# A two-layer encoder on one core: norm sums as two fp32r passes of a high and a low part, and a first block loaded and multiplied in small pieces

## The reference

```
h   = RMSNorm(x);  z = h @ W_in -> [q_a | kv_a | k_rope | B | C | conv_in]
attention on low-rank q and kv (both normed), conv = B * conv3(C * conv_in)
mix = concat(norm per head(attn), norm per group(conv)) @ W_out
x  += RMSNorm(mix)
x  += RMSNorm(W_down relu(W_up RMSNorm(x))^2)
x  += RMSNorm(sigmoid(RMSNorm(x) @ W_g) * (p[i] @ W_p))
```

## Time and profile before

| | |
|---|---|
| time, median of 3 runs | 2851.69 us (2851.42 to 2854.39) |
| the profiled execution | 2853.73 us, its span 2851.9 us |
| PE busy | 2794.9 us, 98% of the span |
| DVE, ACT busy | 1716.5 us (60%), 1203.5 us (42%) |
| share of PE in the chain that ended last | 93% |
| mean granted clock of PE | 0.995 |

### The profile page before, as it was taken

The page is one execution under the profiler, slowest core; times in us unless marked ns, Lnnn a source line. Parts: engine busy times, 40 slices in busy tenths (PEclk is TensorE's granted clock), DMA queues, the critical chain, the costliest instruction groups (busy, mean ns, idle before and its releaser), DMA issues.

```text
span 2851.9 us, 34891 instructions
## 1 busy us (share of the span) xinstructions
PE 2794.9 (98%) x13184; PEld 2307.4 (81%) x13184; DVE 1716.5 (60%) x2300; ACT 1203.5 (42%) x1917; POOL 114.2 (4%) x105
## 2 busy tenths in 40 slices
PE   6999999999999999999999999999999999999996
PEld 5888888888888888888887888888888888888885
DVE  4367888465444544458765588883844454444776
ACT  4236778553111211226643377774621121121473
POOL 0221000000000000000013200000000000000000
PEclk9999999999999999999999999999999999999998
DMA  4121111521111111112332111133211111111232
GB/s 150 60 74 48 32 31 26 212 79 52 59 44 44 57 39 51 45 66 97 103 109 74 57 39 33 28 137 114 88 52 44 44 56 40 51 44 44 76 102 74
DMA packets 62731, 190.73 MB, mean 67 GB/s; under 512 B 7968, under 2 KB 7968, under 8 KB 62624
## 3 DMA queue, kind: packets, MB, share of 16 engines
q1 hardware_dynamic: 62624, 189.29, 20.0%
HBM read 166.13 MB, written 23.13 MB: 66 GB/s over the span
## 4 chain that ended last, share of the span: by engine, by line
PE 93%; ACT 2%; DMA 2%; DVE 2%; SPq 1%; issue 1%; ACTq 0%; DVEq 0%
PE ps L825 28%; PE ps L827 28%; PE ps L826 28%; PE ps L992 3%; PE ps L1017 2%; PE ps L1016 2%; DMA raw<-w_units 1%; DMA mix_lo<-yl 1%; PE ps L1026 1%; PE ps L871 0%; PE ps L893 0%; PE ps L864 0%; ACT hh L1261 0%; ACT pr L1441 0%; PE ps L957 0%
## 5 line engine op out<-in xcount | busy, mean ns | idle before, releaser
L825 PE MATMUL ps<-hh,wh 128*128 128x512 f32 x2192 | 871.6, 398 | 28.1 <-DVE wl L1649 24.2
L827 PE MATMUL ps<-hh,wl 128*128 128x512 f32 x2192 | 855.5, 390 | 0.0
L826 PE MATMUL ps<-hl,wh 128*128 128x512 f32 x2192 | 855.4, 390 | 0.0
L825 PEld LDWEIGHTS ps<-hh,wh 128*128 128x128 f32 x2192 | 412.9, 188 | 122.7 <-issue 31.4
L826 PEld LDWEIGHTS ps<-hl,wh 128*128 128x128 f32 x2192 | 413.0, 188 | 93.1 <-issue 8.6
L827 PEld LDWEIGHTS ps<-hh,wl 128*128 128x128 f32 x2192 | 412.7, 188 | 86.6
L1261 ACT ACTIVATE wh<-raw 128x1024 fp32r<-128x1024 f32 x244 | 254.8, 1055 | 382.7 <-PE ps L827 369.9
L1992 DVE TENSOR_TENSOR xf<-xf,ps 128x512 f32<-128x512 f32 x464 | 310.7, 684 | 146.1 <-PE ps L827 145.5
L825 PE MATMUL ps<-gh,wh 128*128 128x512 f32 x1024 | 398.6, 389 | 0.0
L827 PE MATMUL ps<-gh,wl 128*128 128x512 f32 x1024 | 398.4, 389 | 0.0
L826 PE MATMUL ps<-gl,wh 128*128 128x512 f32 x1024 | 398.3, 389 | 0.0
(11 more groups left out here) (139 smaller groups left out, 3021.6 us busy)
## 6 DMA issues: line engine op xcount, KB each, us to landing
raw<-w_units SPq DMA_DIRECT2D x240, 512.0 KB, 3.3
hh<-mix_hi SPq DMA_DIRECT2D x14, 512.0 KB, 6.2
hl<-mix_lo SPq DMA_DIRECT2D x14, 512.0 KB, 7.0
stage<-w_head SPq DMA_DIRECT2D x16, 320.0 KB, 3.0
xf<-x_in SPq DMA_DIRECT2D x4, 1024.0 KB, 9.0
mix_hi<-cyh SPq DMA_DIRECT2D x8, 512.0 KB, 2.6
mix_lo<-cyl SPq DMA_DIRECT2D x8, 512.0 KB, 3.8
sq<-sums SPq DMA_DIRECT2D x32, 128.0 KB, 2.8
```

The lines of the kernel that those rows point to most:

```text
L825: nc.tensor.matmul(dst, ah, bh, start=start, stop=False)
L826: nc.tensor.matmul(dst, ah, bl, start=False, stop=False)
L827: return nc.tensor.matmul(dst, al, bh, start=False, stop=stop)
```

## The change

Three things are done.

First, 28 norm sums are no longer one float32 matmul but two fp32r matmuls, of the total's high part and its low part (`two_passes`). For each one ACT gets a copy of the total (`post_high`, `pre_high`, or a copy in the input stage), and behind it DVE a subtraction (`post_low`, `pre_low`). They are seven border norms in layer 0 (the table `TWO_PASSES`), five in layer 1 (the two that only serve a next layer or its own end stay as they were), and in each layer four latent sums and four of the convolution. `STATS_AT` is the same as before; only latent sum 1 moves one output later (`LSTAT_AT` 17 to 18, with its neighbours).

Second, the first block is done in pieces. SP loads units 2 and 3 into the idle buffer `bb` beside units 0 and 1, x comes in quarters of a half between them, and the constants come behind. PE works through units and chunks in eight pieces by `first_part`, with the norm sum ahead of the last 36 matmuls. The squares of x (t = 0) are taken after all chunks.

Third, the ones come through a small copy on DVE (`ones_r`), and waits on `w_in` count one load less, since two loads go past `raw`.

```
+TWO_PASSES = [("post", 0, 0), ("pre", 0, 0), ("post", 0, 1), ("pre", 0, 1), ("pre", 1, 1), ("pre", 2, 0), ("post", 2, 1)]
-LSTAT_AT = [15, 17, 21, 23]
+LSTAT_AT = [15, 18, 21, 23]
@@ MIX_ACT
-copy_out.7 square_out.7 copy_out.8 square_out.8 copy_out.9 square_out.9 high.30 post.0.0 copy_out.10
+copy_out.7 square_out.7 copy_out.8 square_out.8 copy_out.9 square_out.9 high.30 post_high.0.0 post.0.0 copy_out.10
...
@@ sync
-            load(0, 0)
-            load(0, 1)
-            sp.dma_start(cst[:, :, :], consts).then_inc(const_in, 16)
-            load_x(0)
-            load(0, 2)
-            load(0, 3)
-            for i in range(1, 4):
-                load_x(i)
+            load(0, 0)
+            load_x(0)
+            load(0, 1)
+            load_x(1)
+            load_beside(0)
+            load_x(2)
+            load_beside(1)
+            load_x(3)
...
@@ tensor
+            def two_passes(dst, ones, hi, lo):
+
+                nc.tensor.matmul(dst, ones.bitcast(f32r), hi, start=True, stop=False)
+                return nc.tensor.matmul(dst, ones.bitcast(f32r), lo, start=False, stop=True)
...
             def post_stats(L, k, t):
...
-                nc.tensor.matmul(ps[:, 6, :], ones, accy[:, t, :], start=True, stop=True).then_inc(post_stat, 1)
+                total = total_at(L, "post", k, t)
+                if total:
+                    pe.wait_ge(total_lo, total)
+                    two_passes(ps[:, 6, :], ones_r[:, 0, :], rpre_r[:, 1, :], accy_r[:, t, :]).then_inc(post_stat, 1)
...
-                    side_by_side([(n, n) for n in range(SLOTS)], 0, pre_ready(R, 0), in_out)
+                    first_part(0, range(2))
+                    first_part(1, range(2))
+                    first_part(0, range(2, 4))
+                    first_part(1, range(2, 4))
+                    first_part(2, range(4))
+                    first_part(0, range(4, DC)).then_inc(in_out, 1)
+                    first_part(1, range(4, DC)).then_inc(in_out, 1)
+                    pe.wait_ge(const_in, 48)
+                    pe.wait_ge(stage_lo, 1)
                     pre_stats(L, -1, 0)
+                    first_part(2, range(4, DC)).then_inc(in_out, 1)
+                    first_part(3, range(DC)).then_inc(in_out, 1)
@@ scalar
+            def high_of_total(L, kind, k, t):
+
+                group = (L + 1, "pre", -1, t) if (kind, k) == ("pre", 2) else (L, kind, k, t)
+                act.wait_ge(*sum_at(last_of(*group)))
+                copy(rpre_r[:, t if kind == "pre" else 1, :], sum_of(group + (0,))).then_inc(total_hi, 1)
@@ vector
+            def low_of_total(L, kind, k, t):
+
+                dve.wait_ge(total_hi, total_at(L, kind, k, t))
+                part = (sum_r if kind == "pre" else accy_r)[:, t, :]
+                whole = (xacc, tmp)[t][:, :] if kind == "pre" else accy[:, t, :]
+                low(part, whole, rpre_r[:, t if kind == "pre" else 1, :]).then_inc(total_lo, 1)
```

More of the change, by code:

```diff
@@ L118 @@
 CHUNKS = CONV // P
+FIRST_AT = [0, 2, 4, 6]
+TWO_PASS = 2
 def taker_of(w):
@@ L836, in unit_output, with first_part @@
                 return last
[L838 to L846, removed]
+            def first_part(n, part):
+                unit_ready(0, n)
+                for k in part:
+                    pe.wait_ge(pre_lo, pre_at(0, -1) * 16 + k + 1)
+                    last = split_product(ps[:, n, :], wh[:, n, k, :], wl[:, n, k, :],
+                                         hh[:, k, hs(0)], hl[:, k, hs(0)], k == 0, k == DC - 1)
+                return last
             def two_tiles(bank, slot, m, moving_hi, moving_lo, start=True, stop=True):
@@ L863, in pre_stats @@
                     pe.wait_ge(pre_ln, pre_at(L, k) * 2 + 1)
-                nc.tensor.matmul(ps[:, 7, :], ones, (xacc, tmp)[t][:, :], start=True, stop=True).then_inc(pre_stat, 1)
+                total = total_at(L - 1, "pre", 2, t) if k < 0 else total_at(L, "pre", k, t)
+                if total:
+                    pe.wait_ge(total_lo, total)
+                    two_passes(ps[:, 7, :], ones_r[:, 0, :], rpre_r[:, t, :], sum_r[:, t, :]).then_inc(pre_stat, 1)
+                else:
+                    nc.tensor.matmul(ps[:, 7, :], ones, (xacc, tmp)[t][:, :], start=True, stop=True).then_inc(pre_stat, 1)
             def post_stats(L, k, t):
@@ L870, in post_stats @@
                     pe.wait_ge(post_ln, post_at(L, k) * 2 + 1)
-                nc.tensor.matmul(ps[:, 6, :], ones, accy[:, t, :], start=True, stop=True).then_inc(post_stat, 1)
+                total = total_at(L, "post", k, t)
+                if total:
+                    pe.wait_ge(total_lo, total)
+                    two_passes(ps[:, 6, :], ones_r[:, 0, :], rpre_r[:, 1, :], accy_r[:, t, :]).then_inc(post_stat, 1)
+                else:
+                    nc.tensor.matmul(ps[:, 6, :], ones, accy[:, t, :], start=True, stop=True).then_inc(post_stat, 1)
             def stats_at(L, *where):
@@ L1344, in _ @@
             for c in range(DC):
-                if c % 4 == 0:
-                    split_unit(0, c // 2)
-                    split_unit(0, c // 2 + 1)
+                if c in FIRST_AT:
+                    split_unit(0, FIRST_AT.index(c))
                 if c == 0:
-                    act.wait_ge(const_in, 32)
+                    act.wait_ge(gains_first, 16)
                 pre_chunk(None, -1, 0, c)
+            for c in range(DC):
+                square((0, "pre", -1, 0, c), x[:, 0, c, :])
             for L in range(DEPTH):
@@ L1383, in _ @@
                                 square((L, "lora", i, i // 2, c), zr[:, c, hs(i // 2)])
+                    for i in range(4):
+                        if LSTAT_AT[i] - 1 == n:
+                            act.wait_ge(*sum_at(last_of(L, "lora", i, i // 2)))
+                            if i == 0:
+                                act.wait_ge(pre_stat, pre_at(L, -1) * 2 + 2)
+                            copy(sum_r[:, i % 2, :], accy[:, i % 2, :]).then_inc(lr_sum_hi, 1)
                     for j in range(CHUNKS - 1):
@@ L1388, in _ @@
                                 nc.scalar.activation(cvs[:, t2, :], cv[:, hs(t2)], ACT.Square).then_inc(cv_sq, 1)
+                            for t2 in range(2 if j < TWO_PASS else 0):
+                                act.wait_ge(cv_sq, L * 8 + 2 * j + t2 + 1)
+                                copy(cvr_r[:, t2, :], cvs[:, t2, :]).then_inc(cv_sq_hi, 1)
                         if CSTAT_AT[j] + 1 == n:
@@ L1830, in _ @@
                             conv_gate(j)
+                        if MULT_AT[j] + 1 == n and j < TWO_PASS:
+                            for t2 in range(2):
+                                dve.wait_ge(cv_sq_hi, L * 2 * TWO_PASS + 2 * j + t2 + 1)
+                                low(cvs_r[:, t2, :], cvs[:, t2, :], cvr_r[:, t2, :]).then_inc(cv_sq_lo, 1)
+                    for i in range(4):
+                        if LSTAT_AT[i] - 1 == n:
+                            dve.wait_ge(lr_sum_hi, L * 4 + i + 1)
+                            low(accy_r[:, i % 2, :], accy[:, i % 2, :], sum_r[:, i % 2, :]).then_inc(lr_sum_lo, 1)
                     if n == 33:
```

147 lines of the change are left out of this document (98 added, 49 removed).

## The result

The changed kernel takes 2830.06 us (median of 4 runs, 2828.62 to 2831.45), the kernel before in the same comparison 2852.56 (4 runs, 2851.42 to 2854.39). The ratio is 0.9920, interval 0.9903 to 0.9938. The forecast was 2830.7.

What follows compares the result with a forecast made beforehand. PE was taken to bound the kernel. Span 2851.9 - 19.1 (first block) - 11.7 (sums) + 9.5 (stalls) + 0.3 = 2830.9, 21.0 less; on the median, 2830.7 us. Own range 2827 to 2835, over the cases 2824 to 2841.

Steps and rivals of the forecast that it cites:

- four stalls: First post norm (t = 0) 3.2 us and MLP pre norm (t = 1) 1.55 us, in both layers: 9.5 us lost.
- unit 4's first matmul earlier: End of the first block: unit 4 starts at 33.5 instead of 49.68, 16.2 us gained.
- clock behind the first block: Behind the first block PE no longer idles, so the clock should not fall: 2.9 us more gained.
- 28 two-pass sums: Border norms, latent and convolution sums: 0.45 us instead of 0.87, gain 0.42 each, 11.7 us in all.
- small rest: First convolution sums: PE may wait for their parts, no more than 0.3 us per layer; 0.3 added in the sum.
- What bounds the kernel: Whole kernel: PE busy 2794.9 of 2851.9 us; its listed waits were two for a low weight part, 24.2 us.
- The rival by which the pairs save nothing: All 28 sums: two passes as dear as one float32 matmul, 2842.4 us; chance 0.03.
- the one by which each pair is waited for: All 28 sums: each waits 1.55 us, 43.4 lost against 30.8 gained, 2864 us; chance 0.03.
- The clock behind a stall: First post norm, both layers: rival that the clock falls in the new stall, 2.9 us each, 2836.5 us; chance 0.09.
- The first block: Kernel start: PE starts at about 8.2, has data throughout and no idle before unit 4; 19.1 us gained with the clock.
- the margin of the ones: First norm sum: its wait for ones_r and the constants has the smallest margin of the start, 1.9 us.
- The rule of the Trainium skill that was set against this part: First block: a stream stopping for a transfer at every tile falls to the lower clock, so pieces would not reach 2.4 GHz.

Runs made afterwards that it cites:

- both parts ahead: Changed kernel with post_high.0.0, post_low.0.0 and pre_low.0.1 moved ahead of high.30, low.30 and value.2.0 in both layers; 2816.62 us, ratio 0.9872.
- the norm sum last: Changed kernel with the input's first norm sum behind the first block's last piece, not ahead of its last 36 matmuls; 2836.50 us, ratio 0.9942.

## Why the prediction was right, and where two errors cancelled

The differences below are from the trace of the changed kernel against that of before, at the same product matmul. Only at the four stalls, where two or three effects fall together, are they taken apart by the experiments: the price of the sums is from the kernels with all sums plain and with both parts ahead, the clock's from the two waits behind which it stayed up.

| term | forecast | measured |
|---|---|---|
| unit 4's first matmul earlier | -16.2 | -17.2 |
| clock behind the first block | -2.9 | -2.9 |
| 28 two-pass sums | -11.7 | -12.4 |
| four stalls | +9.5 | +10.4 |
| clock behind two of the stalls | 0 | +3.2 |
| unit 25's split | not seen | -4.4 |
| small rest: convolution in the forecast, attention in the trace | +0.3 | -0.8 |
| sum | -21.0 | -24.1 (the span: -24.0) |

**What bounds the kernel** held. Each jump in the difference of the traces is one in PE's waits, in the price of a sum, or in its clock. But the list of PE's waits was not as short as the prediction has it. The kernel before had these too:

```profile
PE ps L871 <- DVE accy L1679: 7.5, 1, 7.5
PE ps L825 <- ACT pr L1441: 5.8, 6, 2.1
```

The first is at the kernel's end and did not change; the second is where unit 25's split counts. The last row but one of the table lies in waits for `kl` in the attention, which move by 0.3 us each even between two executions of the changed kernel; it is not explained further.

**Two-pass sums.** Right in kind and a little too small. A pair takes two ordinary steps, 0.45 us, at 24 places of the changed kernel and at all 28 with both parts ahead. The plain sum costs 0.91, not the 0.87 that was read from the earlier trace rows: the reading ended at 120.10, and the next eight matmuls still stand slightly wider apart than 0.227. In the kernel before:

```profile
122.17 0.39 PE L827 MATMUL ps<-hh,wl 128*128 128x512 f32 x1
```

From 118.09 to here are 14 ordinary distances and the sum: 4.08 - 14 x 0.2267 = 0.91 (0.2267 is the 0.68 / 3 of the earlier trace rows unrounded), and the traces with and without two passes come to rest 0.45 apart. In the convolution, where plain sums stand in pairs, the gain is 0.42 to 0.43 each. The rival by which the pairs save nothing is out, and so is the one by which each pair is waited for.

**The stalls.** The step was right in place and cause, and nearly in size. PE's starts stand 3.55 and 1.86 us apart (560.68 to 564.22, 643.22 to 645.08), so 3.32 and 1.63 are lost at once where 3.2 and 1.55 were forecast. The first matmuls behind a wait also stand slightly wider apart, so that by the traces the places cost 3.4 and 1.8 in the end. Here is the first, in the changed kernel:

```profile
560.68 0.39 PE L871 MATMUL ps<-hh,wl 128*128 128x512 f32 x1
561.16 1.06 ACT L1332 ACTIVATE wh<-raw 128x1024 fp32r<-128x1024 f32 x1 [4.24 <-PE ps L871]
562.12 0.61 ACT L1332 ACTIVATE rpre_r<-accy 128x512 fp32r<-128x512 f32 x1
562.25 1.22 DVE L1743 TENSOR_TENSOR wl<-raw,wh 128x1024 fp32r<-128x1024 f32 x1 [4.60 <-ACT wh L1332]
563.39 0.68 DVE L1743 TENSOR_TENSOR accy_r<-accy,rpre_r 128x512 fp32r<-128x512 f32 x1
...
564.22 0.60 PE L901 MATMUL ps<-rpre_r,ones_r 128*128 128x512 f32 x1 [3.16 <-DVE accy_r L1743]
...
564.62 0.63 PE L902 MATMUL ps<-accy_r,ones_r 128*128 128x512 f32 x1
```

The rows show the whole chain: ACT stands idle for 4.24 us before the unit's copy, which waits for an output of PE, the high part stands behind it, DVE does the unit's low part first, and PE waits for the last of them. And the second:

```profile
643.22 0.39 PE L871 MATMUL ps<-hh,wl 128*128 128x512 f32 x1
643.64 0.69 DVE L2088 SCALAR_TENSOR_TENSOR stage<-ps,rpre 128x512 f32<-128x512 f32 x1 [3.09 <-PE ps L871]
644.25 0.68 DVE L1743 TENSOR_TENSOR sum_r<-tmp,rpre_r 128x512 fp32r<-128x512 f32 x1
...
645.08 0.47 PE L901 MATMUL ps<-rpre_r,ones_r 128*128 128x512 f32 x1 [1.47 <-DVE sum_r L1743]
```

**The clock behind a stall** is the step that failed in kind. The forecast took 0 and gave the mechanism a chance of 0.09 as a rival, since no row told of a shorter idle stretch than 4.78 us. It came true in both layers; the pair behind the first stall is shown with 0.60 and 0.63 us a matmul, where an ordinary one has 0.39. Its price was too high, though: 3.68 - 9 x 0.227 = 1.6 us in the stretch, and 1.6 against each of the two waits behind which the clock stayed, not 2.9, because the lower clock lasted 3.4 us here and 6.8 at the earlier trace rows. Over all traces with the wait of 3.16 us (the changed kernel twice, and three experiments) the clock fell behind 9 of 10 such waits. Behind the waits of 1.5 us it did not fall in the changed kernel. The trace of before could have told that much, though no more: it has a wait of 2.07 us, in the row for `pr` that the prediction left out, and behind it the clock stayed at 1.00:

```profile
1917.74 0.47 PE L825 MATMUL ps<-hh,wh 128*128 128x512 f32 x1 [2.07 <-ACT pr L1441]
```

**The moved split of unit 25** is the step that was left out. It was in the diff of the lists, and the wait was in the trace of before (PE waited 5.8 us for `pr` in six places), but I had gone through the lists only for the 28 sums. It gains 4.4 us; together with the clock's 3.2 lost it leaves the total near the forecast by accident. The smaller misses, 1.0 us too little for the first block, 0.7 for the sums and 0.9 for the stalls, partly cancel as well, and that the median came nearer to the forecast than the span did is the spread of single executions.

**The first block.** Right in each step but the length of the slow spell: start at 8.08 (8.2), no idle time before unit 4, which had 3.3 us to spare (its low part ended at 29.15), as forecast. The 1.0 us on top is 0.9 of clock and 0.1 of the start: I took over the 5.5 us at the lower clock from the earlier trace rows, and it was 3.4 here. How long it lasts changes from kernel to kernel with the same first block (see the end), so this gain is in part one of this execution. The wrong number is the margin of the ones, 0.6 us instead of 1.9, which is the smallest now. They came as forecast (22.8, and 22.5 in the forecast); it was the norm sum that stood 1.0 earlier, for the same reason. The rule of the Trainium skill that was set against this part (TensorE: Matmul & The Clock Gate, section on HAM oscillation) speaks of a stream that stops at every tile; no piece stopped here, so its case did not arise. Where a stream did stop once, at the post norm and in the kernel with the norm sum last, the clock behind it mostly fell, which agrees with the direction of that rule (granted clock 0.54 over 3.68 us, 0.50 over 4.93).

## What to carry to other kernels

Where a sum or a product on the busiest engine is made cheaper by preparing its operand elsewhere, look at what stands ahead of the preparation on its own engines: an instruction that waits for the busy engine's last output undoes the gain, and moving three words ahead of such instructions brought 13.4 us here. Price an idle stretch of TensorE at its length and at what the clock may take behind it, as a rival with a real chance, not a remote one. And read a long diff to its end against the list of waits: a line that has nothing to do with the headline was worth 4.4 us, and a total that comes out right is no proof that its terms did.

## What the runs showed of the hardware

A plain float32 norm sum of 128x512 costs PE 0.91 us at 2.4 GHz, of which 0.04 show only in the distances of the matmuls behind it, and two fp32r passes cost 0.45.

In these traces the clock did not follow from a wait's length alone: at the same 3.16 us it fell 9 times in 10 (in one kernel behind the first and not the second), at 2.54 us once in two, at 2.07 and below never. Behind the waits of 3.16 and 2.54 us the lower clock lasted 3.4 us in nine of the ten cases in which it fell, and 6.8 in one; with the waits of 4.78 it lasted 6.8. After the first matmul of the kernel it rose at 3.4 us in the changed kernel and 5.5 in the one before, at 3.1 to 4.5 in the other seven traces with the first block in pieces, and at 4.4 in the kernel before with unit 25's split moved, whose first block is that of before. What decides between these was not tried.
